# Expert pairs two to four: tokens gathered by indirect DMA from a DRAM copy instead of by one-hot products

## The reference

```python
logits  = h @ router_w + router_b                  # 256 tokens x 8 experts
top_vals, top_idx = top_k(logits, 2);  top_w = softmax(top_vals)
combine = sum(one_hot(top_idx) * top_w)            # 256 x 8, two non-zero in a row
for e in range(8):                                 # expert: 1024 -> 3584 -> 1024
    y += combine[:, e:e+1] * ((silu(h @ w_gate[e]) * (h @ w_up[e])) @ w_down[e])
x = x + gate_f * y
```

## Time and profile before

| what | us |
|---|---|
| median of three runs | 2712.49 |
| the three runs | 2716.74, 2712.49, 2711.33 |
| the profiled execution's own time | 2713.75 |
| its span, first to last instruction | 2711.9 |
| PE busy in the span | 2642.3 (97%) |
| DVE, ACT, POOL busy | 1009.0, 448.0, 23.0 |
| mean DMA rate over the span | 235 GB/s |
| experts, from the first `gate_up` to the end of the last `down` | 519.6 to 1403 |

### The profile page before, as it was taken

One profiled execution on the slowest core, in us unless ns is written; L12 is line 12 of the kernel. 1 busy time (PEld: TensorE's weight loads), 2 busy tenths in 40 slices (PEclk: granted clock), 3 DMA queues, 4 the chain that ended last, 5 costly groups with the idle time before them and its releaser, 6 DMA issues.

```text
span 2711.9 us, 42263 instructions
## 1 busy us (share of the span) xinstructions
PE 2642.3 (97%) x18928; PEld 1448.9 (53%) x18928; DVE 1009.0 (37%) x2087; ACT 448.0 (17%) x961; POOL 23.0 (1%) x50
## 2 busy tenths in 40 slices
PE   7999999999999999999999998999999999989998
PEld 4568647433433434344344445558886445554883
DVE  3533557311010110101113778746665422273034
ACT  1110011200000010000012534321110023432000
POOL 0000000100000000000000000000000000000000
PEclk8999999999999999999999999999999999999999
DMA  9979855499999999999982341024254341113541
GB/s 316 322 259 327 321 209 186 188 403 405 408 389 409 405 389 409 405 394 404 405 308 96 135 158 61 32 93 155 94 174 151 133 159 62 64 63 113 164 148 72
DMA packets 243940, 636.56 MB, mean 235 GB/s; under 512 B 14532, under 2 KB 96712, under 8 KB 232424
## 3 DMA queue, kind: packets, MB, share of 16 engines
q1 hardware_dynamic: 241960, 628.92, 61.6%
q0 software_dynamic: 1216, 2.76, 0.3%
q10 hardware_dynamic: 576, 2.10, 0.2%
HBM read 629.94 MB, written 5.90 MB: 234 GB/s over the span
## 4 chain that ended last, share of the span: by engine, by line
PE 93%; DVE 3%; ACT 2%; DMA 1%; issue 1%; SPq 0%; DVEq 0%; ACTq 0%
PE banks L1846 21%; PE banks L1866 11%; PE banks L1654 9%; PE banks L1613 9%; PE banks L1733 8%; PE banks L1316 6%; PE banks L1374 6%; PE banks L1213 3%; PE banks L1580 3%; PE banks L1695 2%; PE banks L1173 2%; PE banks L1097 2%; PE banks L946 2%; PE banks L1082 1%; DVE sb_gate_bc L2877 1%; DMA sb_weights<-ada_w 1%
## 5 line engine op out<-in xcount | busy, mean ns | idle before, releaser
L1846 PE MATMUL banks<-sb_weights,sb_arena 128*32 128x512 f32 (+1 forms) x3840 | 371.8, 539 | 0.2 <-ACT sb_arena L2362 0.2
L1846 PEld LDWEIGHTS banks<-sb_weights,sb_arena 128*32 128x32 f32 x3840 | 129.3, 110 | 231.1 <-issue 211.7
L1654 PE MATMUL banks<-sb_hT,sb_weights 128*128 128x256 f32 x1152 | 251.2, 380 | 0.4 <-ACT sb_arena L2281 0.4
L1654 PEld LDWEIGHTS banks<-sb_hT,sb_weights 128*128 128x128 f32 x1152 | 218.2, 190 | 33.2 <-issue 2.9
L1733 PE MATMUL banks<-sb_weights,sb_arena 128*128 128x512 f32 x528 | 229.4, 594 | 1.5 <-ACT sb_gate_bc L1997 1.5
L1846 PE MATMUL banks<-sb_arena 128*32 128x512 f32 (+1 forms) x2304 | 227.3, 539 | 0.0
L3315 DVE TENSOR_TENSOR sb_hT<-sb_hT,banks 128x256 f32<-128x256 f32 (+1 forms) x96 | 37.2, 388 | 484.9 <-ACT sb_hT L2382 470.9
L1866 PE MATMUL banks<-sb_weights,sb_hT 128*32 128x512 f32 (+1 forms) x2240 | 183.1, 486 | 0.0
L1733 PEld LDWEIGHTS banks<-sb_weights,sb_arena 128*128 128x128 f32 x528 | 99.4, 190 | 125.8 <-issue 123.9
L1316 PE MATMUL banks<-sb_weights,sb_hT 128*128 128x512 f32 (+1 forms) x400 | 160.7, 559 | 1.4 <-ACT sb_mod_rows L2112 1.4
L1374 PE MATMUL banks<-sb_hT,sb_weights 128*128 128x512 f32 (+1 forms) x384 | 154.9, 557 | 0.0
(11 more groups left out here) (365 smaller groups left out, 2803.5 us busy)
## 6 DMA issues: line engine op xcount, KB each, us to landing
sb_weights<-moe_w_gate SPq DMA_DIRECT2D x70, 1024.0 KB, 14.3
sb_weights<-moe_w_up SPq DMA_DIRECT2D x70, 1024.0 KB, 17.4
sb_weights<-moe_w_down SPq DMA_DIRECT2D x70, 1024.0 KB, 15.2
sb_weights<-w_mod SPq DMA_DIRECT2D x48, 1024.0 KB, 6.9
sb_weights<-w_ffn_in SPq DMA_DIRECT2D x44, 1024.0 KB, 7.7
sb_arena<-moe_w_gate SPq DMA_DIRECT2D x42, 1024.0 KB, 16.2
sb_arena<-moe_w_up SPq DMA_DIRECT2D x42, 1024.0 KB, 18.3
sb_arena<-moe_w_down SPq DMA_DIRECT2D x42, 1024.0 KB, 15.1
```

The lines of the kernel that those rows point to most:

```text
L1654: mm = pe.matmul(dst, ring[j][:, k, lo:lo + P], hT[:, k, 0:T * P], start=(k == 0), stop=(k == KC - 1))
L1846: mm = pe.matmul(psum[32 * q:32 * q + 32, r % 2, 0:2 * w], ex_hT[:, k, half * CAP + g * GROUP:half * CAP + (g + 1) * GROUP], wts[:, q, :, ...
```

## The change

In the pairs after the first (experts 2 and 3, 4 and 5, 6 and 7), `gather` and most of `choose` fall away. Instead:

- At the start of the experts, after its half of the first `ex_hT`, ACT copies `xn` into two arena buffers `xn_blocks`, its 32-feature strips reordered so that a quarter row (256 floats) holds the features that belong on one strip of 32 partitions. POOL writes them to a DRAM tensor `normed` (two plain DMAs of 512 KB), ahead of the slot list.
- Four more small DMAs bring the slot list back as `fetch_from`, and DVE turns it into quarter-row numbers of `normed` in `send_rows` (two more instructions, and a wait for four more DMAs).
- After sending the rows of expert 0, 2 or 4, POOL waits until the previous tokens have been turned, and then fetches the next pair's: six indirect DMAs, each 128 rows of 1 KB, into six buffers `fetched`.
- After round 11 of expert 1, 3 or 5, DVE waits for the fetched rows, turns them by six 32 x 32 block transposes of 128 x 256 into `ex_hT` (`turn_fetched`), and then DVE and ACT apply scale and shift in place.
- `ex_hT` is laid out group by group, so the lhsT of `gate_up` is a different view of the same size.
- `choose` stays for the first pair, and in expert 5 for the values that the last expert's `pick_w` needs. The overflow batches keep the old way.

```diff
-        ex_hT = view(12288, KC, 2 * CAP)
+        ex_hT = view(12288, 2 * GROUPS, KC, GROUP)
+        by_chunk = ex_hT.rearrange("p g k s -> p k g s")
+        fetched = [view(at, 256) for at in (15360, 15616, 15872, 16128, 13824, 15104)]
+        xn_blocks = [view(14080, D), view(15360, D)]
...
-                        if s == 3 and half and not last:
+                        if s == 3 and half and n_of is None:
                             gather()
...
-                def upper_half():
+                def upper_half(in_place=False):
                     act.wait_ge(gathered, c.up(gathered, 2))
                     for k in range(KC // 2, KC):
-                        ins = act.activation(ex_hT[:, k, :], psum[:, 4 + k // 2, (k % 2) * 2 * CAP:(k % 2 + 1) * 2 * CAP],
+                        ins = act.activation(by_chunk[:, k, :, :], by_chunk[:, k, :, :] if in_place else gather_bank(k),
...
                 upper_half()
+                if not batch:
+                    for t in range(TX):
+                        act.activation(xn_blocks[t].rearrange("p (b k c) -> p k b c", b=4, c=STRIP),
+                                       xn[:, t, :].rearrange("p (k b c) -> p k b c", b=4, c=STRIP), ACT.Copy).then_inc(xn_blocked, 1)
...
-                dve.wait_ge(listed, 16 * (2 * TX + 6))
+                dve.wait_ge(listed, 16 * (2 * TX + 10))
+                link(TS(fetch_from[:, :, :], fetch_from[:, :, :], SEQ - 1, None, ALU.bitwise_and))
+                TS(fetch_from[:, :, :], fetch_from[:, :, :], 4.0, route_ids[:, 18:19], ALU.mult, ALU.add)
...
+                def turn_fetched(pair):
+                    dve.wait_ge(rows_fetched, 16 * (TX + 2 * GROUPS * pair))
+                    for n in range(2 * GROUPS):
+                        ins = dve.transpose(ex_hT[:, n, :, :].rearrange("p k s -> p (k s)"), fetched[n])
+                    ins.then_inc(gathered, 2)
...
-                        if r == 5 and half and not last:
-                            choose(e + 2)
+                        if r == 5 and half and (scatters or n == E_ - 3):
+                            choose(e + 2, scatters)
...
                     if half and not last:
-                        lower_half()
+                        if not scatters:
+                            turn_fetched(n // 2 + 1)
+                        lower_half(not scatters)
...
+            for t in range(TX):
+                pool.wait_ge(xn_blocked, t + 1)
+                pool.dma_start(normed[t * P:(t + 1) * P, :], xn_blocks[t]).then_inc(rows_fetched, 16)
             pool.wait_ge(rest_in, REST)
...
+            by_group = by_slot.rearrange("(g s) e -> s g e", s=GROUP)
+            for q in range(4):
+                pool.dma_start(fetch_from[STRIP * q:STRIP * (q + 1), :, :], by_group).then_inc(listed, 16)
...
+                if e % 2 == 0 and e < E_ - 2:
+                    pool.wait_ge(gathered, e + 2)
+                    for n in range(2 * GROUPS):
+                        at = fetch_from[:, n % GROUPS, e + 2 + n // GROUPS:e + 3 + n // GROUPS]
+                        pool.indirect_dma_start(fetched[n], None, blocks, row_of(at)).then_inc(rows_fetched, 16)
```

More of the change, by code:

```diff
@@ L347, in program @@
         send_to = sb("send_to", [P, 2, E_], I32)
+        fetch_from = sb("fetch_from", [P, GROUPS, E_], I32)
+        normed = nc.dram_tensor("normed", (SEQ, D), F32, kind="Internal").ap()
         y_back = view(15360, D)
@@ L480, in program @@
         y_sent = sem("y_sent")
+        rows_fetched = sem("rows_fetched")
+        xn_blocked = sem("xn_blocked")
         y_back_in = sem("y_back_in")
@@ L515, in slot_of, with gather_bank @@
             return first[i] if i < len(first) else (1, 2, 0, 3)[(i - len(first)) % SLOTS2]
+        def gather_bank(k):
+            return psum[:, 4 + k // 2, (k % 2) * 2 * CAP:(k % 2 + 1) * 2 * CAP].rearrange("p (g s) -> p g s", s=GROUP)
         def expert_slot(e, s):
@@ L1846, in gate_up @@
                                 mm = pe.matmul(psum[32 * q:32 * q + 32, r % 2, 0:2 * w],
-                                               ex_hT[:, k, half * CAP + g * GROUP:half * CAP + (g + 1) * GROUP],
+                                               ex_hT[:, half * GROUPS + g, k, :],
                                                wts[:, q, :, :, :],
@@ L2385, in expert @@
                     if half and not last:
-                        upper_half()
+                        upper_half(not batch)
                 if batch:
@@ L3268, in weigh, with choose @@
                     ins.then_inc(chosen, 1)
-                def choose(e):
+                def choose(e, picks=True):
                     for t in range(TX):
@@ L3276, in choose @@
                     link(ins, moe_link)
+                    if not picks:
+                        return
                     for t in range(TX):
@@ L3290, in choose_second, with lower_half @@
                     weigh(1)
-                def lower_half():
+                def turn_fetched(pair):
[3 more added lines that the diff above has]
+                    ins.then_inc(gathered, 2)
+                def lower_half(in_place=False):
                     dve.wait_ge(gathered, c.up(gathered, 2))
                     for k in range(KC // 2):
-                        ins = TS(ex_hT[:, k, :], psum[:, 4 + k // 2, (k % 2) * 2 * CAP:(k % 2 + 1) * 2 * CAP],
+                        ins = TS(by_chunk[:, k, :, :], by_chunk[:, k, :, :] if in_place else gather_bank(k),
                                  acol[:, 1, 1, 0, k:k + 1], shift_col(1, 1, k, 0), ALU.mult, ALU.add)
@@ L3340, in expert @@
                         dve.wait_ge(y_sent, 32 * n)
+                    if first:
+                        dve.wait_ge(rows_fetched, 16 * TX)
                     TT(ex_y[:, 0, :], psum[:, 2, :], gate_rows, ALU.mult)
@@ L3431, in row_of @@
                 return bass.IndirectOffsetOnAxis(ap=ap, axis=0)
+            halves = sent_y.rearrange("r (n c) -> (r n) c", n=2)
+            quarters = sent_y.rearrange("r (n c) -> (r n) c", n=4)
+            blocks = normed.rearrange("r (n c) -> (r n) c", n=4)
+            for t in range(TX):
+                pool.wait_ge(xn_blocked, t + 1)
+                pool.dma_start(normed[t * P:(t + 1) * P, :], xn_blocks[t]).then_inc(rows_fetched, 16)
             pool.wait_ge(rest_in, REST)
@@ L3445, in _ @@
                 pool.dma_start(slot_dest[STRIP * q:STRIP * (q + 1), 1, :], by_slot[64:CAP, :]).then_inc(listed, 16)
+            by_group = by_slot.rearrange("(g s) e -> s g e", s=GROUP)
+            for q in range(4):
+                pool.dma_start(fetch_from[STRIP * q:STRIP * (q + 1), :, :], by_group).then_inc(listed, 16)
             pool.wait_ge(list_ready, 2)
[L3447 to L3448 removed]
+            pool.wait_ge(rows_fetched, 16 * TX)
             for e in range(E_ - 1):
```

## The result

The changed kernel takes 2723.2 us (median of 5 runs, 2720.8 to 2727.7) against 2713.0 (5 runs beside them): a ratio of 1.0037, 95% interval 1.0026 to 1.0047. It is slower by some 10 us, past the forecast of 2711.2 and just past the range's end of 2722. Its profiled execution took 2720.8, span 2719.0, against the 2711.9 of before: 7.1 of the 10 us can be looked for in the traces.

The account below looks back on a forecast made before the run. TensorE held the chain, the DMA engines having some 2 us in 222 to spare and becoming the floor. Pairs +0.6, margin -2.4, start +0.5 gave -1.3 us: median 2711.2, likeliest 2708 to 2720, 8 in 10 2703 to 2722.

Parts of the forecast that it names:

- The bound: In the experts, a pair's floor passes from TensorE to the DMA engines; of 5.4 us only 1.8 can be had.
- Rival A: In the experts, the DMA engines have more in them, so the whole 16.3 us are won: 2696.2 us; chance 0.13.
- The fetches: In each later pair, six indirect DMAs, 0.79 MB, take 2.0 us of the DMA engines, out of the weights' time.
- Rival B: In the pairs, fetching scattered rows is dear, 6.9 us a pair instead of 2.0: 2725.9 us; chance 0.17.
- The pairs' term: A pair of experts needs 222.4 us of the DMA engines against 222.2 before: +0.6 us for three pairs.
- The start: At the experts' start, copies and POOL's write are mostly hidden and the slot list comes later: +0.5 us, bounds 0 and 3.1.
- rival C: In expert 0, the slot list comes late, so DVE and TensorE stand 6 us: 2717 us; chance 0.05.
- The margin: Near the end, expert 7's twelfth load can be waited for 2.4 us sooner; all taken: -2.4 us, bounds 0 and -2.4.
- The hiding: Between pairs, some 6 us of transposes and scaling hide under `down`, and POOL's fetches land well before they are wanted.

Follow-up runs that it names:

- fewer weights: 1.97 MB less of weights loaded for each expert: in the changed kernel 2700.4 us, in the kernel before 2710.7 us.
- cut gathers: Kernel before with 2 of 16 products left in each gather of pairs two to four, no copy or fetch: 2711.4 us against 2714.2.
- dead branch: Changed kernel with 32 more products in TensorE's overflow branch, which is never taken: 2718.1 us against 2714.4 of before.
- whole packet of dead code: Changed kernel with 128 products, an estimated 16 KB of code, in TensorE's never-taken overflow branch: 2722.8 us, ratio 1.0033.

## Why the prediction was wrong, step by step

**The bound: right.** The pair's floor passes from TensorE to the DMA engines, with waits for landings, a share of 1.02 to 1.03 and the dips gone. The fewer weights and the cut gathers show it from both sides. Rival A, that 406 GB/s was only TensorE's demand, falls: no slice of the page passes 408. The Trainium skill (HBM Reference, section Specifications (TRN2)) gives some 425 GB/s for a core that streams alone. No slice of the profile's page shows that here, and what was measured decides.

**The fetches: right.** Predicted 2.0 us a pair. The queue shows 2.0 (from 0.9% to 1.8%), and the last loads of an even and the following odd expert lie 112.5 us apart instead of 110.3: 2.2. Rival B's 6.9 us falls. That they come out of the weights' time is shown by the run that fetched once: where they are gone, the loads of an expert land in 110.3 and 110.0 us again. The Trainium skill (DMA: Bandwidth & Descriptors, section Issuing engines are not separate DMA queues) says of DMAs from different engines that they run on the same 16 DMA engines and interleave. The trace agrees.

**The pairs' term: too small.** Predicted +0.6 us for the three, measured +3.1: the last loads of experts 0 and 6 lie 669.5 us apart, against 666.4. (The last landing of expert 6 is missing in the trace of after. It is put 5.1 us behind the landing ahead of it, as in experts 1, 4 and 5: an estimate.) That is 223.2 a pair, not 222.4. Some 0.2 to 0.3 a pair is the fetches. The rest is the other half: I took 110.2 us for every expert whose loads have no dip, and without dips those between an odd and the next even expert took 111.8, 110.2 and 110.1, on the mean 110.7: of the 111.9 of before 1.2 came back a pair where 1.7 was counted. The excess lies in the first of the three alone; the trace shows the engines full there, and its cause was not isolated.

**The start: too small.** Predicted 0.5. The last load of expert 0 lands 1.6 us later, 0.45 of which is there before the change acts: 1.15, inside its bounds. POOL's write and list fall into 521 to 547, mostly beside engines with little to do, as predicted (0.20 against 0.02); the list's last reads leave at 545 to 547, far ahead of 586, so rival C falls.

**The margin: right.** The twelfth load of expert 7 lands at 1344.2 instead of 1339.1, 5.1 later, and the end of the experts is 2.7 later: 2.4 us of margin were used up, as said.

Together 1.15 + 3.1 + 0.4 (expert 7 up to its twelfth load) - 2.4 = +2.2 for the experts, against a forecast of -1.3. With that alone the kernel would stand within the 0.2% that can't be told from no change.

**The hiding: right.** DVE's turning and POOL's fetches cost nothing on the path: TensorE waits between pairs for landings alone. POOL issues six fetches in 633 to 640, 0.94 to 1.01 us each.

**The step that decided it is not in the prediction.** The sum was made of terms inside the experts, as if all behind them stayed. So the time behind the experts was put at nothing without a reason. But the change makes and drops instructions of TensorE, so all later code moves, and behind a jump it may begin at another place of a packet. There stood a gap of 4.46 us in the trace of before, with no more to it than "issue". It should have been asked what it was and whether a change of code can double it. It did: +4.3 us, shown by the dead branch, which takes them back while the experts keep their time (2718.1 us, inside the stated range), and by the whole packet of dead code, which leaves them. The result is thereby 2.2 (experts) + 4.3 (code) + 0.45 (ahead of the change) = 7.0 of the 7.1 us between the profiles; the other 3 of the medians were told above.

## What to carry to other kernels

Where an engine and the transfers are both full, work taken off the engine comes back as waits; ask first for the places where the transfers still rest, and move the freeing of buffers there (873 us for 886 here). Read each idle time that ends with "issue" at a jump as a price: code comes through the DMA engines beside the weights, and an edit ahead can turn one such gap into two. So before an edit of 5 us is judged good or bad, shift its code with a dead branch; and keep the transfers away from the jump, if that is free.

## What the runs showed of the hardware

- At the jump over the branch TensorE stands 1.6 to 2.6 us a gap with the DMA engines at rest (share 0.03) and 4.4 to 5.0 us with weights moving (0.33 and more over the gap). Code arrives in packets of 16 KB, and TensorE goes on 1.3 to 1.7 us behind a packet's end. Kernels that ran only two or three products before the next packet paid twice.
- A gap of 4.4 us goes with the lower clock (1.2 GHz) for 3.4 to 20.5 us; one of 2 us with none in both kernels that had a single one.
- Indirect reads of 1 KB rows from DRAM cost little more than their bytes: 0.79 MB took 2.0 us of the engines, at the weights' own rate, and set the weights' landings back by 2.2 us.
